# Two gated layers that turn unscaled rows and apply the row factor after the product; a norm and a copy moved inside the attention steps

## Chip, cores and metric

One core of one Trainium2 chip runs the whole program in one launch. The metric is the device time of that launch in microseconds (us); lower is better. The engines are named as the profile names them: PE (TensorE, the matrix engine; PEld is its weight load), ACT (ScalarE), DVE (VectorE), POOL (GpSimd) and SP (SyncE, which issues most of the DMAs).

## What is computed

Two transformer-like blocks on 256 tokens of width 1024, all in float32. The parts that matter here:

```
def rmsnorm(x, g):                       # y = x * rsqrt(mean(x*x) + EPS) * g
def swiglu(h, w_gu, w_down):
    gu = h @ w_gu                        # 1024 -> 2 x 2816
    g, u = jnp.split(gu, 2, axis=-1)
    return (jax.nn.silu(g) * u) @ w_down
f = swiglu(rmsnorm(h, ffn1_pre_g), ffn1_w_gu, ffn1_w_down);  h = h + 0.5 * rmsnorm(f, ffn1_post_g)
m = hybrid_mixer(rmsnorm(h, mix_pre_g), ...);                h = h + rmsnorm(m, mix_post_g)
c = memory_cross_attention(rmsnorm(h, xa_pre_g), ...);       h = h + rmsnorm(c, xa_post_g)
f = swiglu(rmsnorm(h, ffn2_pre_g), ffn2_w_gu, ffn2_w_down);  h = h + 0.5 * rmsnorm(f, ffn2_post_g)
```

Then a second block: another mixer and a layer that picks experts for each token. The hybrid mixer projects its input, runs a stick-breaking attention over 16 heads and a state-space scan beside it, normalises each (the state-space output `y * silu(z)` in two groups of 512), and multiplies both by `w_out`.

## The kernel before

**Products.** Tokens stand in two tiles of 128 (`tt` = 0, 1), the width in eight slices of 128 (`kt`). Every weight is streamed once from HBM by SP in 532 blocks of 128x1024 (512 KB) into a ring of four slots (`RING`). Each block is split in two: ACT copies it to `w_high` in PE's fast fp32r form (`split`, L496), DVE writes the rest to `w_low` (`split`, L1005), and PE does three products for each pair of operands (L1750 to L1752: high by high, low by high, high by low). SP loads a slot again as soon as `w_low` of the block in it is done (`w_split`).

**Entering a layer.** `pre_square` (ACT, L512) squares a tile of rows and sums it, then takes the root; `scaled` (DVE, L1027 and L1029) inverts that and writes the rows times the factor to `XN`; `turn_tile(k, tt)` (PE, L1757) turns the eight 128x128 squares of a tile of `XN` into PSUM; `highs` (ACT, L533) multiplies by the gain column and writes `xT_high`, `lows` (DVE, L1039) writes `xT_low`. `k` numbers the norms: 0 is the first gated layer, 3 the state-space norm, 6 the second gated layer. Before a norm that follows a residual update, `post_square` (ACT, L582) and `post_add` (DVE, L1084, L1090, L1092) norm the product in PSUM and add it to `H`, one tile after the other; `h_done` counts the updated tiles.

**The gated layer.** `ffn_up` makes eleven panels of 256 gates and 256 values. PE's first panel goes tile by tile (`panel_by_tile`): tile 0 through four weight blocks, then tile 1; `turn_after` says behind which block of tile 0 the second tile is turned (`None`: both are turned ahead of it). For each panel ACT writes `silu(gate)` (L549) and DVE multiplies by the value (L1055); PE turns the result back one panel later.

**The attention steps.** For `k` = 0 to 9, PE does `scores(k)` (L1924), `suffix_sums(k-1)` (L1941 to L1947), `weighted_values(k-2)` (L1959 to L1961), and half a panel of the projections that are still to come (panels 8 to 10 behind steps 1, 3 and 5; panel 9 holds keys that `scores(4)` needs). `attention_half(k, fill)` is the same step on ACT and on DVE, with one weight block split at `fill(0)` and one at `fill(1)`. On DVE it ends with `softplus_low` (L1192), for which `suffix_sums` waits. The state-space output is finished between these steps: `gated` (DVE, L1334) multiplies by the silu of `z`, the squares (ACT, L512), `scaled` and `panel(8)` follow step 1, `highs` and `lows` of norm 3 follow steps 2 and 3, and `panel(9)` comes behind those of step 3. `XN` and the scratch tile `XDD` share memory.

Every engine works through its own instructions in the order written, and semaphores tie them together.

Of the kernel before, what the change touches and what calls it, by code (L numbers as in the profile page):

```python
# [69 lines left out]

GATE_SCALE = 2.0 ** 14
# [32 lines left out]
def build(nc, stream, w_dt, cols, small_row, rows, x, mem, keys, out):  # L104
# [31 lines left out]
    STAT = sb("stat", [P, 64], 93.75)  # L136
    XAK = sb("xa_kT", [P, 8, SEQ], 97)
# [169 lines left out]
    eps_ok, rms_ok, xn_ok = sem("eps_ok"), sem("rms_ok"), sem("xn_ok")  # L307
# [44 lines left out]
    def _(sp):  # L352
        sp.dma_start(H[:, 0, :], x[0:P, :]).then_inc(x_in, 16)
        sp.dma_start(H[:, 1, :], x[P:SEQ, :]).then_inc(x1_in, 16)
        sp.dma_start(RING[:, 0, :], stream[0]).then_inc(loaded[0], 16)
        sp.dma_start(COLS[:], cols).then_inc(const_in, 16)
        for n in range(1, SLOTS):
            sp.dma_start(RING[:, n, :], stream[n]).then_inc(loaded[n], 16)
# [20 lines left out]
    def _(pool):  # L379
# [4 lines left out]
        pool.dma_start(ROWG[:], rows[0].partition_broadcast(P)).then_inc(row_in, 16)  # L384
# [4 lines left out]
        for mask, sign, compare, fill in ((UPTO, 1, ALU.is_ge, 0.0), (FROM, -1, ALU.is_ge, 0.0),  # L389
# [4 lines left out]
                               pattern=[[sign, P]], channel_multiplier=-sign).then_inc(masks_ok, 1)  # L394

# [60 lines left out]
        pool.wait_ge(xn_ok, 18)  # L456
# [29 lines left out]
    def _(act):  # L486
# [54 lines left out]
        def ffn_up(stage, f):  # L541
# [3 lines left out]
            def silu(p, parity, dyn=None):  # L545
                act.wait_ge(w_used, at(b + PB * (p + 1), dyn, PB))
                if dyn is not None or e + p >= 2:
                    act.wait_ge(hidden_done, at(e + p - 1, dyn))
                act.activation(SG[:, parity, :, :],  # L549
                               PAIR[parity].rearrange("p (t n) -> p t n", t=TT)[:, :, 0:256],  # L550
                               ACT.Silu).then_inc(silu_done, 1)
# [8 lines left out]
            split(b + PB, PB)  # L560
            silu(0, 0)
# [39 lines left out]
        act.wait_ge(eps_ok, 1)  # L601
        act.wait_ge(x_in, 16)
# [3 lines left out]
        split(0, 1)  # L606
        act.wait_ge(const_in, 16)
        highs(0, "ffn1", 0)
        split(1, 1)
        highs(0, "ffn1", 1)  # L610
        split(2, 2)
# [29 lines left out]

        def attention_half(k, fill):
# [8 lines left out]
            fill(1)  # L651
            if k < 8:
# [345 lines left out]
    def _(dve):  # L998
# [33 lines left out]

        def lows(k, gain, tt, high=XTH, low=XTL):
# [13 lines left out]
        def ffn_up(stage, f):  # L1047
            b, e = BASE[stage], f * FFN_PANELS

            def hidden(p, parity, dyn=None):  # L1050
                dve.wait_ge(silu_done, at(e + p + 1, dyn))
                if dyn is not None or e + p >= 2:

                    dve.wait_ge(ht_ps, at(e + p - 1, dyn))
                dve.tensor_tensor(HN[:, parity, :, :], SG[:, parity, :, :],  # L1055
                                  PAIR[parity].rearrange("p (t n) -> p t n", t=TT)[:, :, 256:512],
                                  ALU.mult).then_inc(hidden_done, 1)
# [7 lines left out]
            split(b + PB, PB)  # L1065
            hidden(0, 0)
# [46 lines left out]
        dve.wait_ge(x_in, 16)  # L1113
        scaled(0, H, 0)
        dve.wait_ge(x1_in, 16)
        scaled(0, H, 1)
        split(0, 1)
# [43 lines left out]

        def attention_half(k, fill):
# [159 lines left out]
        panel(7)  # L1322
# [1107 lines left out]
```

## Time and profile before

| | |
|---|---|
| median of 3 runs | 1722.03 us (1719.54 to 1722.96) |
| profiled execution | 1721.7 us, span 1720.0 us |
| mean granted TensorE clock | 0.989 of 2.4 GHz |
| busy share of the span | PE 97%, PEld 86%, DVE 69%, ACT 54%, POOL 7% |
| HBM | 284.86 MB read, 166 GB/s over the span |

The span is the profiled part of one execution. Times in the rows are us from its start. A row of the timeline gives start, duration, engine, line, operation, tiles, and in brackets how long the engine had been idle before it and what ended that.

### The profile page before, as it was taken

To read this page: it belongs to the slowest core of one execution; us is meant where nothing else is said; L and a number is where in the kernel's file an instruction comes from. 1 tells how busy PE (TensorE), PEld (TensorE's weight loads), DVE (VectorE), ACT (ScalarE), POOL (GpSimd) and SP (SyncE) were. 2 spreads that over 40 slices of the span, in tenths; PEclk is the share of its full clock that TensorE was granted. 3 is DMA by queue.
4 is the path that set the end of the run, shared out by engine and by line. 5 is a ranking of instruction groups with operands and counts; after the bars stand their busy time and mean duration, and the time that the engine had idled before them with its cause. 6 is when DMAs were issued, how large, how long until landed. Compare 5 with 4: busy or idle time off the path is not lost.

```text
span 1720.0 us, 30593 instructions
## 1 busy us (share of the span) xinstructions
PE 1672.3 (97%) x10346; PEld 1482.4 (86%) x10346; DVE 1190.6 (69%) x1827; ACT 934.2 (54%) x1540; POOL 114.5 (7%) x106
## 2 busy tenths in 40 slices
PE   7999999989998999999989999999999999999998
PEld 6888898889897788879979999999999888888887
DVE  5555687487666555466664799989999866666664
ACT  5445546476655544456354444467777654455554
POOL 0000004000000000010010000112222200000000
PEclk9999999989999999999999999999999999999999
DMA  7555453323453555645344455444444365665663
GB/s 260 186 183 183 171 196 123 111 97 124 153 190 123 171 183 184 192 144 187 125 163 158 161 169 195 169 162 146 147 147 148 132 209 193 195 193 190 192 194 122
DMA packets 78814, 286.79 MB, mean 167 GB/s; under 512 B 8864, under 2 KB 9120, under 8 KB 78624
## 3 DMA queue, kind: packets, MB, share of 16 engines
q1 hardware_dynamic: 77888, 282.27, 49.4%
q0 software_dynamic: 864, 3.67, 0.6%
q8 instruction: 41, 0.67, 0.2%
q14 instruction: 21, 0.17, 0.0%
HBM read 284.86 MB, written 1.05 MB: 166 GB/s over the span
## 4 chain that ended last, share of the span: by engine, by line
PE 79%; DVE 10%; issue 6%; ACT 4%; DVEq 1%; DMA 0%; ACTq 0%; POOL 0%; SPq 0%; POOLq 0%
PE ps L1750 24%; PE ps L1752 24%; PE ps L1751 24%; DVE one_at_key L1653 3%; DVE w_low L1005 3%; ACT gate_high_at_key L931 1%; DVE gate_low_at_key L1670 1%; ACT w_high L496 1%; PE ps L1757 1%; PE ps L1839 1%; DVE xT_low L1039 0%; DVE tmp L1090 0%; ACT xn L512 0%; PE ps L2276 0%; DVE h L1092 0%
## 5 line engine op out<-in xcount | busy, mean ns | idle before, releaser
L1005 DVE TENSOR_TENSOR w_low<-ring,w_high 128x1024 fp32r<-128x1024 f32 x532 | 654.2, 1232 | 341.4 <-ACT w_high L496 339.3
L496 ACT ACTIVATE w_high<-ring 128x1024 fp32r<-128x1024 f32 x532 | 559.4, 1056 | 319.2 <-PE ps L1752 312.4
L1750 PE MATMUL ps<-xT_high,w_high 128*128 128x256 f32 x1600 | 462.1, 289 | 1.9 <-DVE xT_low L1039 1.9
L1751 PE MATMUL ps<-xT_high,w_low 128*128 128x256 f32 x1600 | 454.2, 284 | 0.0
L1752 PE MATMUL ps<-xT_low,w_high 128*128 128x256 f32 x1600 | 454.1, 284 | 0.0
L1750 PEld LDWEIGHTS ps<-xT_high,w_high 128*128 128x128 f32 x1600 | 308.2, 193 | 5.9 <-DVE w_low L1005 2.3
L1751 PEld LDWEIGHTS ps<-xT_high,w_low 128*128 128x128 f32 x1600 | 308.4, 193 | 0.7 <-issue 0.5
L1752 PEld LDWEIGHTS ps<-xT_low,w_high 128*128 128x128 f32 x1600 | 308.0, 193 | 0.0
L1750 PE MATMUL ps<-w_high,expert_w_high 128*128 128x512 f32 x512 | 200.5, 392 | 0.4 <-DVE expert_w_low L1713 0.4
L1751 PE MATMUL ps<-w_high,expert_w_low 128*128 128x512 f32 x512 | 200.0, 391 | 0.0
L1752 PE MATMUL ps<-w_low,expert_w_high 128*128 128x512 f32 x512 | 200.0, 391 | 0.0
L1750 PE MATMUL ps<-w_high,xT_high 128*128 128x512 f32 x464 | 187.1, 403 | 11.5 <-DVE xT_low L1039 6.4
L1752 PE MATMUL ps<-w_low,xT_high 128*128 128x512 f32 x464 | 183.4, 395 | 0.0
L1751 PE MATMUL ps<-w_high,xT_low 128*128 128x512 f32 x464 | 183.4, 395 | 0.0
L980 ACT ACTIVATE expert_w_high<-expert_w 128x256 fp32r x124 | 51.8, 418 | 164.9 <-PE ps L1752 164.9
L1750 PEld LDWEIGHTS ps<-w_high,xT_high 128*128 128x128 f32 x464 | 88.7, 191 | 31.5 <-DVE w_low L1005 7.6
L1750 PEld LDWEIGHTS ps<-w_high,expert_w_high 128*128 128x128 f32 x512 | 96.6, 189 | 20.7 <-issue 0.6
L1751 PEld LDWEIGHTS ps<-w_high,expert_w_low 128*128 128x128 f32 x512 | 96.6, 189 | 19.9
L1752 PEld LDWEIGHTS ps<-w_low,expert_w_high 128*128 128x128 f32 x512 | 96.5, 189 | 19.9
L931 ACT ACTIVATE gate_high_at_key<-one_at_key,gate_high 128x128 f16<-128x128 f16 x256 | 82.0, 391 | 52.5 <-DVE one_at_key L1653 52.5
L1731 DVE TENSOR_TENSOR expert_w_low<-expert_w,expert_w_high 128x256 fp32r<-128x256 f32 x124 | 52.7, 425 | 82.3 <-ACT expert_w_high L980 82.3
L1752 PEld LDWEIGHTS ps<-w_low,xT_high 128*128 128x128 f32 x464 | 88.6, 191 | 19.1
(373 smaller groups left out, 2115.1 us busy)
## 6 DMA issues: line engine op xcount, KB each, us to landing
ring<-in_stream SPq DMA_DIRECT2D x532, 512.0 KB, 3.4
row_gain<-in_rows POOLq DMA_DIRECT2D x4, 512.0 KB, 4.4
h<-in_x SPq DMA_DIRECT2D x2, 512.0 KB, 4.3
mem_sb<-in_mem SPq DMA_DIRECT2D x1, 1024.0 KB, 11.3
keys_sb<-in_keys POOLq DMA_DIRECT2D x1, 1024.0 KB, 5.3
out<-result SPq DMA_DIRECT2D x2, 512.0 KB, 2.6
last_gain<-in_rows POOLq DMA_DIRECT2D x1, 512.0 KB, 4.8
cols<-in_cols SPq DMA_DIRECT2D x1, 78.5 KB, 7.4
```

The costliest lines, as they stand in the source:

```text
L496: act.activation(WH[:, n % SLOTS, :], RING[:, n % SLOTS, :], ACT.Copy).then_inc(w_high, 1)
L931: last = act.activation(OAH[:, g % 2, j, :], OAE[:, j // 2, :, j % 2], ACT.Copy, scale=gate)
L980: act.activation(WTH[:, v % 4, :], slot, ACT.Copy).then_inc(wt_high, 1)
L1005: dve.tensor_tensor(WL[:, n % SLOTS, :], RING[:, n % SLOTS, :], WH[:, n % SLOTS, :].bitcast(F32), ALU.subtract).then_inc(w_split, 1)
L1653: dve.tensor_tensor(OAE[:], IOTA16[:].unsqueeze(1).to_broadcast([P, GROUP // 2, P, 2]), pairs(KEY_T[:, 0, :], g, dyn), ALU.is_equal).then_ ...
L1670: dve.tensor_tensor(OAL[:, g % 2, :, :, :], OAE[:], pairs(GATE_LOW, g, dyn), ALU.mult).then_inc(low1_ok, 1)
L1731: dve.tensor_tensor(WTL[:, v % 4, :], slot, WTH[:, v % 4, :].bitcast(F32), ALU.subtract).then_inc(wt_low, 1)
L1750: pe.matmul(out, high, w_hi, start=start, stop=False, skip_group_check=True)
L1751: pe.matmul(out, low, w_hi, start=False, stop=False, skip_group_check=True)
L1752: return pe.matmul(out, high, w_lo, start=False, stop=stop, skip_group_check=True)
L1757: last = pe.transpose(xt_psum(k, tt)[:, kt, :], XN[:, tt, kt * P:(kt + 1) * P], IDENT[:])
L1839: last = pe.transpose(hidden_psum(p)[:, o:o + P], HN[:, parity, tt, ft * P:(ft + 1) * P], IDENT[:])
```

## The change

Four edits.

1. Both gated layers turn the rows of `H` as they are (no `scaled`). The factor of each row, 1/rms, goes to `ROW_FACTOR` (`row_factor` on DVE) and is applied behind the product: as the scale of the silu, and as the scalar of the multiplication that makes `hidden`. As the factor differs from tile to tile, each of the two becomes two instructions of 128x256 for a panel. The squares move behind `highs` of both tiles.
2. The order of the first loads: rows 0, the columns of gains, ring 0, ring 1, rows 1, then ring 2 and 3; the row gain (POOL's queue, 512 KB) waits until ring 3 has landed. The first gated layer turns its second tile behind block 0 of tile 0, the second gated layer behind block 2 (1 before). The splits of weight blocks move ahead of tile 1's `highs` and `lows`.
3. State-space norm: `gated(0)` goes behind `panel(7)`, `gated(1)` into step 0; the squares of tile `k` (`ssd_squares`) come ahead of step k's exponentials for k = 0 and 1, the roots (`ssd_roots`) behind step 1's.
4. `panel(9)`'s copies go ahead of `highs` and `lows` of the state-space norm's second tile.

```diff
@@ sync @@
         sp.dma_start(H[:, 0, :], x[0:P, :]).then_inc(x_in, 16)
+        sp.dma_start(COLS[:], cols).then_inc(const_in, 16)
+        sp.dma_start(RING[:, 0, :], stream[0]).then_inc(loaded[0], 16)
+        sp.dma_start(RING[:, 1, :], stream[1]).then_inc(loaded[1], 16)
         sp.dma_start(H[:, 1, :], x[P:SEQ, :]).then_inc(x1_in, 16)
-        sp.dma_start(RING[:, 0, :], stream[0]).then_inc(loaded[0], 16)
-        sp.dma_start(COLS[:], cols).then_inc(const_in, 16)
-        for n in range(1, SLOTS):
+        for n in range(2, SLOTS):
@@ gpsimd: row_gain's first load, moved behind the masks @@
+        pool.wait_ge(loaded[SLOTS - 1], 16)
         pool.dma_start(ROWG[:], rows[0].partition_broadcast(P)).then_inc(row_in, 16)
@@ scalar: ffn_up @@
-                act.activation(SG[:, parity, :, :],
-                               PAIR[parity].rearrange("p (t n) -> p t n", t=TT)[:, :, 0:256],
-                               ACT.Silu).then_inc(silu_done, 1)
+                for tt in range(TT):
+                    last = act.activation(SG[:, parity, tt, :], PAIR[parity][:, tt * 512:tt * 512 + 256], ACT.Silu,
+                                          scale=ROW_FACTOR[:, tt:tt + 1])
+                last.then_inc(silu_done, 1)
...
             split(b + PB, PB)
+            act.wait_ge(factor_ok, 2 * f + 2)
             silu(0, 0)
@@ scalar: start @@
+        act.wait_ge(const_in, 16)
+        highs(0, "ffn1", 0)
+        split(0, 4)
+        highs(0, "ffn1", 1)
         act.wait_ge(x_in, 16)
         pre_square(0, H, 0)
         act.wait_ge(x1_in, 16)
         pre_square(0, H, 1)
-        split(0, 1)
-        act.wait_ge(const_in, 16)
-        highs(0, "ffn1", 0)
-        split(1, 1)
-        highs(0, "ffn1", 1)
-        split(2, 2)
@@ scalar: attention @@
+        def ssd_squares(tt):
+            act.wait_ge(y_used, 2)
+            act.wait_ge(y_done, tt + 1)
+            for g in range(2):
+                w, n = slice(g * 512, g * 512 + 512), 2 * tt + g
+                chain(act.activation(XN[:, tt, w], YS[:, tt, w], ACT.Square, accum_out=STAT[:, n:n + 1]))
+        def ssd_roots():
+            chain(act.activation(STAT[:, 4:8], STAT[:, 0:4], ACT.Ln, scale=1.0 / 512,
+                                 bias=STAT[:, EPS_COL:EPS_COL + 1]))
+            act.activation(STAT[:, 8:12], STAT[:, 4:8], ACT.Exp, scale=-0.5).then_inc(rms_ok, 2)
...
             fill(1)
+            if k < 2:
+                ssd_squares(k)
...
+            if k == 1:
+                ssd_roots()
...
-            if k == 1:
-                for tt in range(TT):
-                    act.wait_ge(y_done, tt + 1)
-                    pre_square(3, YS, tt, 2, log=True)
-            elif k in (2, 3):
-                highs(3, "ssd", k - 2, YTH)
+            if k == 2:
+                highs(3, "ssd", 0, YTH)
             if k in (1, 3, 5):
                 panel(8 + k // 2)
+            if k == 3:
+                highs(3, "ssd", 1, YTH)
@@ scalar: second gated layer @@
         split(b, 4)
         post_square(2, 0)
-        split(b + 4, 2)
+        split(b + 4, 3)
+        highs(6, "ffn2", 0)
+        post_square(2, 1)
+        split(b + 7, 1)
+        highs(6, "ffn2", 1)
         updated_square(6, 0, 4)
-        post_square(2, 1)
-        highs(6, "ffn2", 0)
         updated_square(6, 1, 4)
-        split(b + 6, 1)
-        highs(6, "ffn2", 1)
-        split(b + 7, 1)
@@ vector @@
+        def row_factor(k, tt):
+            dve.wait_ge(rms_ok, 2 * k + tt + 1)
+            dve.reciprocal(ROW_FACTOR[:, tt:tt + 1], STAT[:, 4 + tt:5 + tt]).then_inc(factor_ok, 1)
...
-                dve.tensor_tensor(HN[:, parity, :, :], SG[:, parity, :, :],
-                                  PAIR[parity].rearrange("p (t n) -> p t n", t=TT)[:, :, 256:512],
-                                  ALU.mult).then_inc(hidden_done, 1)
+                for tt in range(TT):
+                    last = dve.scalar_tensor_tensor(HN[:, parity, tt, :], PAIR[parity][:, tt * 512 + 256:tt * 512 + 512],
+                                                    ROW_FACTOR[:, tt:tt + 1], SG[:, parity, tt, :], ALU.mult, ALU.mult)
+                last.then_inc(hidden_done, 1)
@@ vector: start (both scaled(0, ...) are gone) @@
         dve.wait_ge(const_in, 16)
         lows(0, "ffn1", 0)
-        split(1, 1)
+        split(0, 4)
         lows(0, "ffn1", 1)
-        split(2, 2)
+        row_factor(0, 0)
+        row_factor(0, 1)
@@ vector: attention (gated(0) now stands behind panel(7), ahead of the wait for y_ps 3) @@
                 dve.scalar_tensor_tensor(SPL[:, k % 2, :], ZS[:, k % 2, :], -1.0, ZS[:, k % 2, :],
                                          ALU.mult, ALU.min).then_inc(abs_done, 1)
+            if k == 0:
+                gated(1)
...
             if k == 1:
-                gated(0)
-                gated(1)
-                dve.wait_ge(y_done, 2)
                 scaled(3, YS, 0, 2, log=True)
                 scaled(3, YS, 1, 2, log=True)
-            elif k in (2, 3):
-                lows(3, "ssd", k - 2, YTH, YTL)
+            elif k == 2:
+                lows(3, "ssd", 0, YTH, YTL)
             if k in (1, 3, 5):
                 panel(8 + k // 2)
+            if k == 3:
+                lows(3, "ssd", 1, YTH, YTL)
@@ vector: second gated layer @@
         split(b, 4)
         post_add(2, 0, 1.0)
-        split(b + 4, 1)
-        updated_scale(6, 0, 4)
-        split(b + 5, 1)
+        split(b + 4, 2)
+        lows(6, "ffn2", 0)
+        split(b + 6, 1)
         post_add(2, 1, 1.0)
-        lows(6, "ffn2", 0)
-        updated_scale(6, 1, 4)
-        split(b + 6, 2)
+        split(b + 7, 1)
         lows(6, "ffn2", 1)
+        row_factor(6, 0)
+        row_factor(6, 1)
@@ tensor @@
         def turn_tile(k, tt):
-            pe.wait_ge(xn_ok, 2 * k + tt + 1)
+            if k == 0:
+                pe.wait_ge(ident_ok, 1)
+                pe.wait_ge(x1_in if tt else x_in, 16)
+            elif k == 6:
+                pe.wait_ge(h_done, 5 + tt)
+            else:
+                pe.wait_ge(xn_ok, XN_OK[k] + tt + 1)
+            rows = H if k in (0, 6) else XN
...
-        turn_tile(0, 1)
-        ffn_up("ffn1_up", 0, 0, None)
+        ffn_up("ffn1_up", 0, 0, 0)
...
-        ffn_up("ffn2_up", 1, 6, 1)
+        ffn_up("ffn2_up", 1, 6, 2)
```

## Rows read from the trace of the kernel before

**Rows 1.** Waits of PE over the whole span: us in total, times, longest.
```profile
PE ps L1757 <- DVE xn L1029: 13.6, 5, 7.5
PE ps L1750 <- DVE xT_low L1039: 8.3, 4, 3.3
PE ps L1750 <- DVE w_low L1005: 5.3, 4, 2.6
```

**Rows 2.** Timeline of the start.
```profile
4.83 1.06 ACT L512 ACTIVATE xn<-h 128x1024 f32<-128x1024 f32 x1 [2.74 <-DMA h<-in_x]
...
7.52 3.65 PE L1757 MATMUL ps<-ident,xn 128*128 128x128 f32 x16 [7.52 <-DVE xn L1029]
...
8.51 1.06 ACT L496 ACTIVATE w_high<-ring 128x1024 fp32r<-128x1024 f32 x1 [0.84 <-DMA ring<-in_stream]
9.59 2.17 ACT L533 ACTIVATE xT_high<-ps,cols 128x128 fp32r<-128x128 f32 x8
...
10.83 2.16 DVE L1039 SCALAR_TENSOR_TENSOR xT_low<-ps,cols,xT_high 128x128 fp32r<-128x128 f32 x8
...
17.38 0.50 PE L1750 MATMUL ps<-w_high,xT_high 128*128 128x512 f32 x1 [1.54 <-DVE w_low L1005]
```

**Rows 3.** Stretches: length, busy us of PE, PEld, DVE, ACT, POOL, granted clock, DMA share, GB/s.
```profile
368.20:376.80 8.60, 8.60 (x39) 8.60 (x40) 7.50 (x15) 6.50 (x12) 0.00 (x0) 0.50 0.35 124
...
557.70:564.50 6.80, 5.25 (x12) 4.02 (x13) 4.91 (x12) 2.41 (x5) 0.53 (x1) 0.50 0.44 155
...
569.60:577.00 7.40, 7.40 (x33) 6.11 (x34) 4.92 (x11) 3.39 (x4) 0.00 (x0) 1.00 0.30 99
```

**Rows 4.** Timeline of attention steps 0 to 4, by engine: ACT, then DVE, then PE.
```profile
341.76 0.85 ACT L656 ACTIVATE softplus<-softplus 128x768 f32<-128x768 f32 x1 [1.88 <-DVE softplus L1169]
...
343.52 0.96 DVE L1185 SCALAR_TENSOR_TENSOR softplus<-scores,softplus 128x768 f32<-128x768 f32 x1 [1.79 <-ACT softplus L657]
...
353.74 2.35 DVE L1334 TENSOR_TENSOR ssd_out<-ssd_out,projections 128x1024 f32<-128x1024 f32 x2
...
358.99 0.88 DVE L1029 TENSOR_SCALAR xn<-ssd_out,stat 128x512 f32<-128x512 f32 x2 [0.98 <-ACT stat L518]
...
367.13 0.95 DVE L1192 TENSOR_TENSOR softplus_low<-softplus,softplus_high 128x768 fp32r<-128x768 f32 x1
...
368.18 0.66 PE L1944 MATMUL ps<-softplus_high,from_r 128*128 128x384 f32 x1 [4.05 <-DVE softplus_low L1192]
...
372.90 1.91 PE L1757 MATMUL ps<-ident,xn 128*128 128x128 f32 x8
...
382.32 0.71 PE L1924 MATMUL ps<-projections 64*128 64x256 f32 x4 [0.83 <-ACT projections L539]
```

**Rows 5.** Timeline at the entry of the second gated layer, DVE, then PE.
```profile
551.00 1.23 DVE L1092 SCALAR_TENSOR_TENSOR h<-tmp,h 128x1024 f32<-128x1024 f32 x1
...
554.85 1.09 PE L1757 MATMUL ps<-ident,xn 128*128 128x128 f32 x8 [1.51 <-DVE xn L1029]
559.25 0.76 PE L1750 MATMUL ps<-w_high,xT_high 128*128 128x512 f32 x1 [3.30 <-DVE xT_low L1039]
...
569.58 0.50 PE L1750 MATMUL ps<-w_high,xT_high 128*128 128x512 f32 x1 [2.63 <-DVE w_low L1005]
```

**Rows 6.** Page, costliest groups: weight block on DVE, and two of 128x256.
```profile
L1005 DVE TENSOR_TENSOR w_low<-ring,w_high 128x1024 fp32r<-128x1024 f32 x532 | 654.2, 1232 | 341.4 <-ACT w_high L496 339.3
...
L980 ACT ACTIVATE expert_w_high<-expert_w 128x256 fp32r x124 | 51.8, 418 | 164.9 <-PE ps L1752 164.9
...
L1731 DVE TENSOR_TENSOR expert_w_low<-expert_w,expert_w_high 128x256 fp32r<-128x256 f32 x124 | 52.7, 425 | 82.3 <-ACT expert_w_high L980 82.3
```

**Rows 7.** View of the tile silu_gate: ns min/median/max, first and last start.
```profile
L549 ACT ACTIVATE silu_gate<-ps x22: 579/580/597, 28.3 to 690.9; 128x512 f32<-128x512 f32 x22
```

**Rows 8.** Timeline of PE and DVE at the end of the first gated layer.
```profile
144.74 0.60 PE L1839 MATMUL ps<-ident,hidden 128*128 128x128 f32 x4
...
141.32 0.68 DVE L1055 TENSOR_TENSOR hidden<-silu_gate,ps 128x512 f32<-128x512 f32 x1
```

More of the change, by code:

```diff
@@ L68 @@
 HG_CHUNK = 32
+XN_OK = {k: 2 * sum(j not in (0, 6) for j in range(k)) for k in range(9)}
 GATE_SCALE = 2.0 ** 14
@@ L136, in build @@
     STAT = sb("stat", [P, 64], 93.75)
+    ROW_FACTOR = STAT[:, 12:14]
     XAK = sb("xa_kT", [P, 8, SEQ], 97)
@@ L306, in build @@
     act_chain, dve_chain = sem("act_chain"), sem("dve_chain")
-    eps_ok, rms_ok, xn_ok = sem("eps_ok"), sem("rms_ok"), sem("xn_ok")
+    eps_ok, rms_ok, xn_ok, factor_ok = sem("eps_ok"), sem("rms_ok"), sem("xn_ok"), sem("row_factor_ok")
     xt_ps, xt_high, xt_low = sem("xT_psum"), sem("xT_high_done"), sem("xT_low_done")
@@ L383, in _ @@
                            pattern=[[-1, P]], channel_multiplier=1).then_inc(ident_ok, 1)
-        pool.dma_start(ROWG[:], rows[0].partition_broadcast(P)).then_inc(row_in, 16)
         for mask in (UPTO, FROM, BEFORE, CAP, ONES):
@@ L394, in _ @@
                                pattern=[[sign, P]], channel_multiplier=-sign).then_inc(masks_ok, 1)
+        pool.wait_ge(loaded[SLOTS - 1], 16)
+        pool.dma_start(ROWG[:], rows[0].partition_broadcast(P)).then_inc(row_in, 16)
         def row_gain(k):
@@ L455, in _ @@
         pool.wait_ge(iota_ok, 1)
-        pool.wait_ge(xn_ok, 18)
+        pool.wait_ge(xn_ok, XN_OK[8] + 2)
         pool.memset(GE[:, 105:, :], 1.0).then_inc(slots_one, 1)
@@ L1065, in ffn_up @@
             split(b + PB, PB)
+            dve.wait_ge(factor_ok, 2 * f + 2)
             hidden(0, 0)
@@ L1112, in _ @@
         dve.memset(STAT[:, EPS_COL:EPS_COL + 1], EPS).then_inc(eps_ok, 1)
[L1113 to L1117, printed above, removed]
         dve.wait_ge(const_in, 16)
         lows(0, "ffn1", 0)
-        split(1, 1)
+        split(0, 4)
         lows(0, "ffn1", 1)
-        split(2, 2)
+        row_factor(0, 0)
+        row_factor(0, 1)
         dve.wait_ge(small_in, 32)
@@ L1160, in over_diagonals, with gated @@
             return mask[:].unsqueeze(1).unsqueeze(1).to_broadcast([P, 2, 2, P])
+        def gated(tt):
+            dve.wait_ge(y_used, tt + 1)
+            dve.wait_ge(z_silu, 2)
+            y = YS[:, tt, :]
+            dve.tensor_tensor(y.rearrange("p (a n) -> p a n", a=2), y.rearrange("p (a n) -> p a n", a=2),
+                              Z[:, :, tt, :], ALU.mult).then_inc(y_done, 1)
         def attention_half(k, fill):
@@ L1322, in _ @@
         panel(7)
+        gated(0)
         dve.wait_ge(y_ps, 3)
@@ L1328, in _ @@
         dve.tensor_tensor(YS[:, 1, :], YS[:, 1, :], XDD[:], ALU.add).then_inc(y_used, 1)
-        def gated(tt):
-            dve.wait_ge(y_used, tt + 1)
-            dve.wait_ge(z_silu, 2)
-            y = YS[:, tt, :]
-            dve.tensor_tensor(y.rearrange("p (a n) -> p a n", a=2), y.rearrange("p (a n) -> p a n", a=2),
-                              Z[:, :, tt, :], ALU.mult).then_inc(y_done, 1)
         for k in range(10):
@@ L1339, in _ @@
             if k == 1:
-                gated(0)
-                gated(1)
-                dve.wait_ge(y_done, 2)
                 scaled(3, YS, 0, 2, log=True)
                 scaled(3, YS, 1, 2, log=True)
-                dve.wait_ge(xn_ok, 8)
-            elif k in (2, 3):
-                lows(3, "ssd", k - 2, YTH, YTL)
+                dve.wait_ge(xn_ok, XN_OK[3] + 2)
+            elif k == 2:
+                lows(3, "ssd", 0, YTH, YTL)
             if k in (1, 3, 5):
                 panel(8 + k // 2)
+            if k == 3:
+                lows(3, "ssd", 1, YTH, YTL)
             elif k == 7:
@@ L1754, in turn_tile @@
         def turn_tile(k, tt):
-            pe.wait_ge(xn_ok, 2 * k + tt + 1)
+            if k == 0:
[6 more added lines that the diff above has]
+            rows = H if k in (0, 6) else XN
             for kt in range(KT):
-                last = pe.transpose(xt_psum(k, tt)[:, kt, :], XN[:, tt, kt * P:(kt + 1) * P], IDENT[:])
+                last = pe.transpose(xt_psum(k, tt)[:, kt, :], rows[:, tt, kt * P:(kt + 1) * P], IDENT[:])
                 if kt % 4 == 3:
```

## The prediction

> **What bounds the kernel now.** I read the page's busy shares first (PE 97% of the span), then the list of what PE waited for, then the timeline around each wait that the diff touches. PE sets the time, so only PE's idle time, and stretches in which its clock is low, can be won. Three rows of waits hold most of that idle time: on `xn`, on `xT_low` and on `w_low`, 27.2 us in all [rows 1]; a fourth, before `suffix_sums(2)`, is 4.05 us [rows 4]. Beside them stands a cost that no wait shows: after a gap PE runs at the lower of its two clock levels, 1.2 GHz. PE idled 4.05 us, and from there to 376.8 the granted clock is 0.50; at the entry of the second gated layer it idled 1.51 and 3.30 us within six, and 557.7 to 564.5 is at 0.50 [rows 3, 5].
>
> **Unit costs.** PE at full clock starts a 512-wide product about every 0.227 us (7.40 us hold 33 of them [rows 3]); six of them, one weight block for one token tile, take 1.36 us, and a first panel (48) 10.9 us. Eight turns take about 0.9 us at full clock (1.09 with the drain of the last [rows 5]) and twice that at 0.50 (1.91 [rows 4]). Eight `highs` take 2.17 us, eight `lows` 2.16, a `w_high` 1.06, a `w_low` 1.23, of which 1.15 before the next can follow [rows 2, 6].
>
> **Start.** Before, rows 0 land at 4.83, squares, root, inverse and `scaled` put the first turn at 7.52, and the first block's `w_high` waits for ring 0 until 8.51. The panel runs without a gap only from 17.38, when 12 of its 48 products are done, so it ends at 17.38 + 36 x 0.227 = 25.5 [rows 2].
> After: no scaling. Rows 0 now share the engines with less (the row gain and rows 1 come later), so they land at 4.3 to 4.8; turns follow, four turns at 1.2 GHz are 0.9 us, `highs` of tile 0 run from 5.6 to 7.8, `w_high` of blocks 0 to 3 to about 12.0, and `w_low` of block 0 is done at 10.2. DVE's chain then is 1.15 us a block, to 13.7. PE does block 0 from 10.2, turns tile 1, and finds every block ready behind it. At full clock it would end at 10.2 + 10.9 + 0.9 + about 1.2 of waits = 23.2, a gain of 2.3. The columns' DMA (78.5 KB, now second in SP's queue) has to be there by 5.6; it is small and has one transfer ahead of it. Rows 1 and the three blocks need 2.1 MB more by 11.5; 4.5 us of this kernel's 400 GB/s and more would carry it, so they are in time. The row gain waits on POOL's queue, with only the waits for `h_done` and the state-space work of much later behind it.
> But the clock: the 16 turns of before take 3.65 us, 0.23 us each, the price of the lower level, while the first product at 11.6 already runs at full rate. In the new order PE works 1.8 us, idles some 3.5, then starts block 0. I take block 0 and the second turns at 1.2 GHz (1.36 + 0.9 = 2.3 us more at most) and 1.0 us of it net, since part of it fills the waits for `w_low`. Gain 1.3 us; bounds 0.3 and 2.5.
> The Trainium skill ("TensorE: Matmul & The Clock Gate", "What's actually happening") says that the throttled level is the default and that activity releases it. The trace agrees (0.23 us a turn at the start, 0.11 later), and by the rule the early turns buy no warm clock, where a reading by waits alone would give 2.3.
>
> **The gated layers' panels.** Silu goes from one instruction of 0.58 us to two, the product with the value from one of 0.68 to two [rows 7]. The nearest 128x256 rows are 0.42 and 0.43 us [rows 6], so +0.26 on ACT and +0.18 on DVE for each of 22 panels, 9.7 us of engine time. On the path it costs nothing: PE turns `hidden` one whole panel (11 us) later, and where the cover is thinnest, the last panel, DVE begins the product at 141.32 and PE wants it at 144.74 [rows 8], 2.7 us after it is done; 0.44 fits. Without that cover it would be 22 x 0.44 = 9.7 us. The squares and the two inverses, about 3 us on ACT, now lie ahead of the second panel's splits: at the start they end by 18 and the panel is wanted at 24; in the second layer they end around 567.1, block 4 is split by 569.3, and PE wants it at 569.3. I count 0.1.
>
> **Attention steps.** Removed from behind step 1 on DVE: `gated` twice (2.35), the wait for the squares and roots, which kept the last `scaled` until 359.9; there remain four half rows of 0.44 (0.88 for two [rows 4]). DVE ends `softplus_low` of step 1 at 353.7 [rows 4], 0.2 later by what comes in step 0; 1.9 of `scaled` and 0.6 of `panel(8)` put its step 2 at 356.5 against 360.5, 4.0 us earlier.
> Where the work goes: `gated(0)` (1.22) into a wait of 0.96 before the carry product, 0.2 left over; `gated(1)` into DVE's wait of 1.79 for the logarithm; the squares of a tile (1.5 us, an estimate from the 1.06 of a row square [rows 2] cut in two with its readouts) into ACT's waits for `abs`, 1.88 in step 0 [rows 4]; the roots (0.6) into ACT's wait before `softplus_high`. So step 0 costs 0.2.
> Step 2's own chain on DVE (block, `abs`, `log_attention`, logarithm, `softplus`, block, `softplus_low`) ran 360.5 to 368.0, 7.5 us; from 356.5 it ends near 363.9. PE wants it at 364.13 (368.18 - 4.05) + 0.2, so the 4.05 us are gone, by 0.4. Before, PE's work from there to `scores(4)` ran 368.18 to 381.49 (382.32 - 0.83), 13.3 us, of which 8.6 at 0.50 [rows 3, 4]; at full clock those are 4.3 and the whole is 9.0: PE is at `scores(4)` at 373.4. Step 3 on DVE takes 2.2 (`lows`) + 7.5 + 0.7 (`panel(9)`, now ahead of the second `lows`), to 374.4, so PE waits 1.0 there (0.83 before). `scores(4)` moves from 382.32 to 374.5. The second `lows` now lie behind it, and `softplus_low` of step 4 is ready 0.4 after PE wants it in step 5. Gain 7.8 - 0.4 = 7.4; bounds 3.5 (half of the stall stays and the clock falls again) and 8.
>
> **Second gated layer.** Before: PE's last product of the layer ahead ends at 553.34 (554.85 - 1.51), its first panel has 48 products and two turns, 12.6 us, so 566.0 is the ideal; it ended at 569.58 + 30 x 0.227 = 576.4. The 10.4 lost are 7.4 of waits (1.51 + 3.30 + 2.63) and the stretch at 0.50 [rows 3, 5].
> After: `h` of tile 0 is ready at 552.2 [rows 5], before PE is free, so the turn starts at 553.34; `highs` 554.0 to 556.2; `lows` from 555.2, the first two slices at 555.8: block 0 starts at 555.9, not 559.25. Blocks 0 and 1 follow on; block 2's `w_low` stands behind the `lows` on DVE and is done at 558.6, when PE arrives; PE is through it at 560.0. `post_add` of tile 1 stands behind that `w_low`: 558.6 + 0.2 + 1.25 + 1.25 = 561.3. PE waits 1.35, turns until 562.2, waits 0.3 for block 3 (`w_low` behind `post_add`), and ends tile 0 at 563.9; tile 1 has its first `lows` at 563.8. End 563.9 + 5.4 = 569.3, less the 0.1 above. Gain 7.0; bounds 4 (the clock falls at these shorter gaps as well, 1.7 a time, and the second turn is late) and 8.
>
> **Sum.** 1.3 + 7.4 + 7.0 = 15.7 us. The profiled execution took 1721.7 (span 1720.0), so 1706.0; the median of the runs lies 0.3 above it: 1706.3. The low-clock stretches in places that the diff leaves alone shift with the rest; one more or one fewer is worth some 2 us.
>
> **Rivals.**
> - *The stall in the attention steps only moves.* For it: my margin is 0.4 us, and DVE is busy 7.50 of 8.60 us behind the stall [rows 3]; steps 3 and 4 hold the same work. Then PE waits some 2 us before `suffix_sums(2)` or at `scores(4)` and the clock falls again: 3.5 instead of 7.4, 1710.2.
> - *The second gated layer keeps part of its loss.* For it: two waits of 1.7 and 1.35 remain, and 1.51 and 3.30 were followed by 6.8 us at 0.50. Against it: the gap of 2.63 at 567 was followed by 7.40 us at 1.00 [rows 3, 5]. It costs 3: 1709.3. With the first rival, 1713.2. The Trainium skill (same page, "HAM oscillation — how this bites in real kernels") tells of short bursts between waits that keep PE falling back to the low clock; the trace has one case of each kind.
> - *The halved silu and product are exposed.* 9.7 us, 1716.0. Against it: the slack of 2.7 us [rows 8].
> - *The start or a clock stretch elsewhere comes out better*: 2.5 instead of 1.3 and one stretch of 0.50 fewer, 1702.
> - *Nothing is gained*: the waits on `xn` are replaced by waits on `w_low` of the same length in all three places. 1722. The chain on DVE loses real instructions, which speaks against it.
> - *Slower.* PE turns once, falls idle and begins the panel cold; if the clock stayed at 1.2 GHz, each 2 us would cost 1. The three gains are eaten at 34 us of low clock (15.7 + 1.3, doubled), three panels; at 50 us the time is 1706.3 + 25 - 1 = 1730. For it: at 368.2 PE was busy and yet had 0.50 for 8.6 us [rows 3]. Against it: no stretch here is longer.
>
> **Chances.** Forecast (1702.5 to 1709) 0.56; attention stall moves 0.14; second layer keeps half 0.10; both 0.05; exposed halves 0.03; better 0.06; nothing gained 0.04; slower 0.02. 1700.5 to 1712.8 leaves out most of "both" and the last cases, and a tail of "better", under 2 in 10. A measurement of this kernel tells 0.2% (3.4 us) from no change: faster 0.94, same 0.04, slower 0.02.
>
> **What would show it.** Right: `silu_gate` and `hidden` with 44 instructions of about 0.42 us; no wait of PE on `xn` at the start or near 545; first product at about 10, first panel done near 24; no wait over 1 us at `suffix_sums(2)`; no 0.50 between 364 and 377; `scores(4)` some 9 us earlier in the span; 15.9 us from the last product ahead of the second gated layer to its first panel's end (23.0 before). Wrong: waits on `w_low` in those places, ACT idle behind `y_used` in step 0, or low clock in the first two panels or after the 1.35 us gap.

## The result, and the profile after

The changed kernel took 1707.15 us (median of five runs, 1706.76 to 1713.11) against 1722.03 (1719.54 to 1723.5): a ratio of 0.9928, 95% interval 0.9909 to 0.9946. Two further series gave 1706.42 (0.9922, 0.9909 to 0.9936) and 1710.63 (0.9936, 0.9922 to 0.9950). The forecast was 1706.3, with a range of 1702.5 to 1709: the first two medians lie in it, the third lies 1.6 above it. The profiled execution took 1707.15, span 1705.4, 14.6 us shorter than the span before.

All 16 runs of the changed kernel lie in two groups: nine at 1706.3 to 1707.2 with a mean granted clock of 0.993 or 0.994, seven at 1710.4 to 1713.1 with 0.989 to 0.992. Their cause is taken up with the experiments.

What PE waited for, over the whole span (us in total, times, longest):

```profile
PE ps L1777 <- DVE xT_low L1066: 6.5, 3, 2.6
PE ps L1792 <- DMA h<-in_x: 4.8, 1, 4.8
PE ps L1792 <- DVE xn L1051: 4.6, 3, 2.6
...
PE ps L1777 <- DVE w_low L1027: 4.0, 2, 3.9
...
PE ps L1958 <- ACT projections L545: 1.0, 1, 1.0
...
PE ps L1792 <- DVE h L1121: 0.9, 1, 0.9
```

The wait on `xn` fell from 13.6 us to 4.6 [rows 1] (what is left belongs to other norms), and the wait on `softplus_low` is not in the list any more. New are a wait for rows 0 and one of 0.9 for `h`.

The start, PE and ACT:

```profile
4.79 1.94 PE L1792 MATMUL ps<-ident,h 128*128 128x128 f32 x8 [4.79 <-DMA h<-in_x]
6.00 2.18 ACT L539 ACTIVATE xT_high<-ps,cols 128x128 fp32r<-128x128 f32 x8 [3.90 <-PE ps L1792]
...
10.60 0.79 PE L1777 MATMUL ps<-w_high,xT_high 128*128 128x512 f32 x1 [3.87 <-DVE w_low L1027]
11.19 0.63 PE L1778 MATMUL ps<-w_high,xT_low 128*128 128x512 f32 x1
...
13.32 1.91 PE L1792 MATMUL ps<-ident,h 128*128 128x128 f32 x8
...
15.56 0.39 PE L1779 MATMUL ps<-w_low,xT_high 128*128 128x512 f32 x1
```

A product takes 0.63 us until 15.3 and 0.39 from there, and a row of eight turns 1.91, as at 0.50 before [rows 4]: block 0 and tile 1's turns ran at 1.2 GHz, as forecast.

The attention steps (PE and DVE) and the entry of the second gated layer (PE, DVE):

```profile
350.49 0.95 DVE L1227 TENSOR_TENSOR softplus_low<-softplus,softplus_high 128x768 fp32r<-128x768 f32 x1
351.35 1.67 DVE L1051 TENSOR_SCALAR xn<-ssd_out,stat 128x512 f32<-128x512 f32 x4
...
360.28 0.95 DVE L1227 TENSOR_TENSOR softplus_low<-softplus,softplus_high 128x768 fp32r<-128x768 f32 x1
361.67 0.44 PE L1978 MATMUL ps<-softplus_high,from_r 128*128 128x384 f32 x1
...
372.00 0.71 PE L1958 MATMUL ps<-projections 64*128 64x256 f32 x4 [1.01 <-ACT projections L545]
...
543.34 1.03 PE L1792 MATMUL ps<-ident,h 128*128 128x128 f32 x8
545.90 0.47 PE L1777 MATMUL ps<-w_high,xT_high 128*128 128x512 f32 x1 [1.54 <-DVE xT_low L1066]
...
549.87 1.23 DVE L1121 SCALAR_TENSOR_TENSOR h<-tmp,h 128x1024 f32<-128x1024 f32 x1
551.15 1.09 PE L1792 MATMUL ps<-ident,h 128*128 128x128 f32 x8 [0.90 <-DVE h L1121]
552.29 0.50 PE L1777 MATMUL ps<-w_high,xT_high 128*128 128x512 f32 x1
```

`softplus_low` of step 2 is done at 361.2, and `suffix_sums(2)` starts at 361.67 without a wait; `scores(4)` waits 1.01 (0.83 before [rows 4]). In the second gated layer the three waits of 1.51, 3.30 and 2.63 [rows 5] are 1.54 and 0.90. And the clock stayed up (stretches: length, busy us of PE, PEld, DVE, ACT, POOL, granted clock, DMA share, GB/s):

```profile
364.20:372.00 7.80, 6.79 (x59) 6.61 (x58) 7.43 (x9) 5.58 (x10) 0.00 (x0) 1.00 0.28 78
...
546.00:553.00 7.00, 6.05 (x29) 4.65 (x30) 6.17 (x11) 3.56 (x10) 0.53 (x1) 1.00 0.57 175
```

**Where the 14.6 us are**, by the shift of one event in each stage between the two traces: ACT's first square behind the first gated layer from 196.20 to 195.17 (1.0); up to the state-space scan 2.6 (so 1.6 more, in a stretch that the diff doesn't touch: 0.50 for 3.4 us from 254.1, where it was 6.8 us from 253.9); behind the attention steps, the next such square from 462.85 to 453.00, 9.85 (7.25 more); the first turn of `hidden` in the second layer from 587.42 to 570.15, 17.3 (7.4 more); and at the last squares from 1708.59 to 1694.03, 14.6: 2.7 given back in the expert layer.

Only 0.9 of those 2.7 us are low clock (6.8 us at 0.50 from 1346.4, where the kernel before has 3.4). Another 1.7 are lost ahead of that, at full clock, on the same 1928 products. The stretch between two of PE's waits for `gate_high_at_key`, the changed kernel and then the kernel before (columns as above):

```profile
1127.50:1343.80 216.30, 213.55 (x1928) 201.66 (x1928) 214.87 (x302) 157.01 (x362) 66.31 (x60) 1.00 0.44 145
1144.60:1359.40 214.80, 212.76 (x1928) 201.66 (x1928) 214.00 (x302) 157.05 (x362) 63.26 (x60) 1.00 0.43 146
```

It takes 216.3 to 216.5 us in all eleven profiles of kernels that turn unscaled rows, and 214.8 to 214.9 in the three that don't (before, kernels 1 and 3 below). So this loss comes with the new gated layers every time, and not with the halved instructions, which kernel 3 has. PE's gaps ahead of the products of `gate_high_at_key` grow by 0.03 to 0.2 us now and then; the diff touches no line of this layer, and what makes them grow stays open.

### The profile page after: what moved, and what is told of

It reads as the page before. It is cut to its first block, busy times and chain, and to the rows that moved or that the text cites. A ratio compares the mean times of both kernels' runs of the same rounds, so it can differ in the third digit from the quotient of the medians.

```text
span 1705.4 us, 30633 instructions
## 1 busy us (share of the span) xinstructions
PE 1667.1 (98%) x10346; PEld 1476.0 (87%) x10346; DVE 1192.4 (70%) x1845; ACT 938.7 (55%) x1560; POOL 117.6 (7%) x106
## 4 chain that ended last, share of the span: by engine, by line
PE 81%; DVE 9%; issue 6%; ACT 3%; DVEq 1%; ACTq 0%; DMA 0%; POOL 0%; POOLq 0%
PE ps L1777 25%; PE ps L1779 25%; PE ps L1778 25%; DVE one_at_key L1680 3%; DVE w_low L1027 2%; ACT gate_high_at_key L953 1%; PE ps L1792 1%; DVE gate_low_at_key L1697 1%; PE ps L1874 1%; ACT w_high L502 0%; DVE xT_low L1066 0%; PE ps L2310 0%; PE ps L2154 0%; PE ps L2016 0%; PE ps L2034 0%
## 6 DMA issues: line engine op xcount, KB each, us to landing
cols<-in_cols SPq DMA_DIRECT2D x1, 78.5 KB, 3.6
```

## The experiments

Kernel 1 is that of experiment 1, and so on; kernel 10 has the narrow products spread as well, kernel 11 has not. All times stand beside runs of the kernel before on the same chip. A stage is measured between the events just named.

**1. Attention edits alone** (edits 3 and 4 on the kernel before).

> The kernel before with edits 3 and 4 alone (state-space norm in steps 0 and 1, panel 9's copies ahead of the second highs and lows). Theory (the three gains add up, each in its own place): 7.2 us faster than before, 1714.5 to 1715, no PE wait over 1.1 us in the attention steps, and no 0.50 stretch between 364 and 377; the PE waits on xn at 7.5 and 553 as in rows 2 and 5. Rival (the steps gained only because the start had shifted the chip's clock stretches): the wait of 4.05 us is gone but a stretch of low clock of 6.8 us or more comes at the wait of 1 us ahead of scores(4), and only 4 us are gained.

Measured: 1715.13 against 1721.73, ratio 0.9965 (0.9952 to 0.9979), 6.6 faster. The stage from the scan to the square behind the attention steps took 126.63 us, 133.86 before, 126.61 in the changed kernel. The theory holds: 7.2 us, independent of the other edits. The profiled execution was the slowest of the five (1718.2, granted clock 0.988); its low clock lies outside the attention steps, none of it between 259 and 548 us.

**2. Gated layers alone** (the changed kernel with edits 3 and 4 undone).

> The changed kernel with edits 3 and 4 undone: unscaled rows, first loads and the new orders in the two gated layers alone. Theory: 1.0 us at the start and 7.3 in the second layer, 8.3 faster than before, 1713.7; the 4.05 us wait ahead of suffix_sums(2) stays, with 8 to 10 us of low clock behind it. Rival (the three places share one gain, since low-clock stretches move between them): under 5 us faster, with more low clock than before outside the attention steps.

Measured: 1713.99, ratio 0.9963 (0.9950 to 0.9977), 7.7 faster, for 8.3 expected. The wait of 4.1 on `softplus_low` is back, and the granted clock is 0.50 for 6.8 us with it (8 to 10 expected). 6.6 + 7.7 = 14.3 of the 15.3 us that the changed kernel had in the same series (1721.73 - 1706.42): the places add up within what the clock leaves uncertain.

**3. The halves alone.**

```diff
-                act.activation(SG[:, parity, :, :], PAIR[parity]...[:, :, 0:256], ACT.Silu)
+                for tt in range(TT):
+                    act.activation(SG[:, parity, tt, :], PAIR[parity][...], ACT.Silu, scale=ROW_FACTOR[:, tt:tt + 1])
...
+        dve.memset(ROW_FACTOR, 1.0).then_inc(factor_ok, 1)
```

The product with the value on DVE is halved in the same way.

> The kernel before with silu and hidden as two instructions of 128x256 for each panel, with a factor of 1.0 for every row (so nothing is normalised in another way). Theory (hidden behind PE): within 1 us of before, ACT and DVE busier by 22 x 0.35 and 22 x 0.27 us, no new wait of PE. Rival (exposed): 22 x 0.6 = 13 us slower if each panel's turn waits, 0.6 to 1.2 slower if only the last panel of each layer does.

Measured: 1721.40 against 1721.73, ratio 1.0001 (0.9992 to 1.0010), 11 runs. The views of the tiles `silu_gate` and `hidden` in this kernel (ns min/median/max):

```profile
L551 ACT ACTIVATE silu_gate<-ps,stat x44: 454/463/475, 28.1 to 690.1; 128x256 f32<-128x256 f32 x44
L1059 DVE SCALAR_TENSOR_TENSOR hidden<-ps,stat,silu_gate x44: 473/477/486, 29.0 to 691.4; 128x256 f32<-128x256 f32 x44
```

Each is 0.05 us dearer than I had taken from 128x256 rows of other operations, 0.35 on ACT and 0.27 on DVE for a panel, and none of it shows: hidden.

**4. Turns of the identity at the start** (on the changed kernel; nobody reads their output).

```diff
+        warm(14)                       # 14 x pe.transpose(PS[:, 1024:1152], IDENT, IDENT)
         turn_tile(0, 0)
+        warm(20)
         ffn_up("ffn1_up", 0, 0, 0)
```

> The changed kernel with turns of the identity that nobody reads: 14 before the first real turn (from 1.6 to about 4.8 us, where PE only waits for rows 0) and 20 between the turns of tile 0 and the first block (from 6.7, where PE waited 3.87 us for w_low). Nothing else changes. Theory (the start's missing 1.3 us of the 2.3 that waits alone would give are low clock, since PE had fallen idle before block 0): block 0 and the second turns run at 2.4 GHz, the first panel ends 1.0 to 1.4 us earlier, 1705.2 to 1705.5 against 1706.4. Rival (the start is bound by w_low and by the second tile's highs, not by the clock): within 0.3 us, with the time moved into waits; or later, where the idle turns are still running when w_low is done.

Measured: 1711.30 (1709.92 to 1711.44), ratio 0.9936. Both expectations missed that. It is also the ratio of the changed kernel's own series on the same chip (1710.63, 0.9936, experiment 8): by medians the turns neither gained nor lost, and a loss stands only against the lower group of the changed kernel's times. PE at the start of this kernel:

```profile
1.60 3.15 PE L1939 MATMUL ps<-ident 128*128 128x128 f32 x14 [1.60 <-POOL ident L387]
4.67 1.07 PE L1792 MATMUL ps<-ident,h 128*128 128x128 f32 x8
5.58 2.35 PE L1939 MATMUL ps<-ident 128*128 128x128 f32 x20
10.03 0.50 PE L1777 MATMUL ps<-w_high,xT_high 128*128 128x512 f32 x1 [2.10 <-DVE w_low L1027]
...
13.84 0.63 PE L1778 MATMUL ps<-w_high,xT_low 128*128 128x512 f32 x1
```

The real turns ran at the higher level (1.07 for eight), but 20 were over at 7.9, PE paused 2.1 us, and the clock fell again at 11.4. Still the first layer ended 0.4 to 1.0 us earlier than in the changed kernel's profiles. What is lost against a profile of the lower group lies far behind it, in places that no edit touches; the granted clock of those stretches:

```profile
250.30:260.50 10.20, 10.20 (x38) 9.04 (x38) 8.26 (x26) 1.07 (x4) 0.00 (x0) 0.50 0.15 51
803.30:806.70 3.40, 3.40 (x18) 3.40 (x17) 3.01 (x11) 0.28 (x1) 0.00 (x0) 0.51 0.45 154
868.10:878.30 10.20, 7.69 (x35) 7.32 (x36) 7.00 (x19) 5.65 (x17) 5.01 (x1) 0.50 0.68 249
```

In the changed kernel's profiled execution the same places have 3.4 us, none, and 6.8:

```profile
254.30:257.70 3.40, 3.40 (x10) 2.69 (x9) 3.24 (x12) 0.46 (x2) 0.00 (x0) 0.53 0.00 0
865.30:872.10 6.80, 4.46 (x22) 4.09 (x21) 5.78 (x16) 4.24 (x12) 4.40 (x1) 0.51 0.64 242
```

By stages, against that execution, it is 3.2 us behind panel 2, 1.8 in the second mixer and 1.0 at the expert layer's entry, with 0.9 won back in the expert layer.

**5. Without edit 4** (panel 9's copies again behind the second tile's `highs` and `lows`).

> The changed kernel with panel 9's copies again behind highs and lows of the norm's second tile. Theory (by the queues: ACT ends those highs about 366.4 + 2.2 and is free before panel 9 is done at 370.9, but DVE would do 2.2 us of lows first, of which it has the inputs only at 368 to 370, behind softplus_low at 371.2): panel 9's copy on DVE at 373.4 instead of 371.2, scores(4) 2.2 us later, 1.5 to 2.2 us slower: 1708.3. Rival (no need of edit 4: DVE has the lows done before panel 9): within 0.3 us.

Measured: 1714.66 (1708.3 expected), ratio 0.9960 (0.9947 to 0.9974); the attention stage took 132.55 us instead of 126.61. Timeline, DVE and PE:

```profile
370.77 2.16 DVE L1066 SCALAR_TENSOR_TENSOR ssd_outT_low<-ps,cols,ssd_outT_high 128x128 fp32r<-128x128 f32 x8
372.85 0.68 DVE L1072 COPY projections<-ps 128x512 f32<-128x512 f32 x1
...
373.63 1.23 PE L1958 MATMUL ps<-projections 64*128 64x256 f32 x4 [3.11 <-issue]
```

The copy starts 1.6 us later than in the changed kernel (372.85 against 371.21, with the start 0.4 earlier), the wait ahead of `scores(4)` is 3.1 instead of 1.0, and then the granted clock is 0.50 for 10.2 us. The expectation had the wait right and left out the clock. In this stage edit 4 is worth 5.9 us, of which the wait is 2.1 and the rest goes with the low clock: without it the stall of before moves by one step, as my first rival had it.

**6. Old order in the second gated layer, rows still unscaled.**

```diff
-        split(b + 4, 3)                 # ACT
-        highs(6, "ffn2", 0)
-        post_square(2, 1)
+        split(b + 4, 2)
+        updated_square(6, 0, 4)
+        post_square(2, 1)
+        highs(6, "ffn2", 0)
...
-        lows(6, "ffn2", 0)              # DVE
-        split(b + 6, 1)
         post_add(2, 1, 1.0)
+        lows(6, "ffn2", 0)
...
-        ffn_up("ffn2_up", 1, 6, 2)
+        ffn_up("ffn2_up", 1, 6, 1)
```

> The changed kernel with the second gated layer's queues in the order of before (post_square and post_add of tile 1 ahead of highs and lows of tile 0, the squares between, second turn behind block 1), but with unscaled rows. Theory (the 7.3 us come mostly of the order, not of the scaling that is gone): tile 0 is turned at 543.3 as in the changed kernel, its lows start only behind post_add of tile 1, first product near 548.5 instead of 545.9, and the second turn is late too: 3 to 5 us slower than the changed kernel, about 1710.5. Rival (it comes of the missing scaling): within 1 us.

Measured: 1717.54 (11 runs, 1712.90 to 1718.66; some 1710.5 expected), ratio 0.9972. From the last square ahead of the layer to its first turn of `hidden`: 39.52 us, against 39.48 before and 32.06 in the changed kernel. Timeline, PE:

```profile
544.08 1.03 PE L1792 MATMUL ps<-ident,h 128*128 128x128 f32 x8
549.48 0.76 PE L1777 MATMUL ps<-w_high,xT_high 128*128 128x512 f32 x1 [4.36 <-DVE xT_low L1067]
...
558.93 0.50 PE L1777 MATMUL ps<-w_high,xT_high 128*128 128x512 f32 x1 [2.65 <-DVE w_low L1028]
```

Turning unscaled rows lets the turn start without a wait and gives nothing by itself: the 1.51 us come back in the wait for `lows`, 4.36 instead of 3.30, with a turn that is done sooner. Those `lows` stand behind `post_add` of tile 1 on DVE. With unscaled rows, then, the order makes all of the 7.4 us. Whether the new order would give as much with scaled rows was not tried, so it isn't shown that the order needs no help from the missing scaling.

The wait of 2.65 at 558.93 shows something more. In the kernel before and in kernel 3 the same wait (2.63) was followed by full clock, and my prediction leaned on that. Here it was followed by low clock, and in kernel 1 too (2.65 at 560.44, then 0.50 from 561.9 to 565.3):

```profile
559.60:563.00 3.40, 3.40 (x10) 2.62 (x9) 1.48 (x8) 0.00 (x0) 0.00 (x0) 0.51 0.42 154
```

**7. Old order of the first loads.**

> The changed kernel with the first loads in the order of before (rows 0, rows 1, ring 0, columns, rings 1 to 3, and the row gain at once on POOL's queue). Theory (the columns land 7.4 us after their issue as in before, near 9.6): highs of tile 0 start 3.6 us later than at 6.0, block 0 at 14 instead of 10.6, while the second tile's turn no longer waits; 2.5 to 3.5 us slower, 1709.4, all the gain of the start and more. Rival (the order of the loads does nothing, ACT and DVE set the pace): within 0.5 us.

Measured: 1713.96 (1709.4 expected), ratio 0.9952. The first layer ended 3.0 us later than in the changed kernel. ACT and PE:

```profile
9.64 2.18 ACT L537 ACTIVATE xT_high<-ps,cols 128x128 fp32r<-128x128 f32 x8 [7.54 <-DMA cols<-in_cols]
...
14.24 0.79 PE L1775 MATMUL ps<-w_high,xT_high 128*128 128x512 f32 x1 [7.54 <-DVE w_low L1025]
```

The columns, 78.5 KB, land 7.3 us after their issue, behind three loads of 512 KB; in the changed kernel, behind one, it is 3.6. Without this edit the start is 2.0 us slower than before (198.16 against 196.20). The row gain is back in POOL's queue at once in this kernel too; the two were not tried apart.

**8. The changed kernel again, twice.**

> The changed kernel once more, for its two groups of times (1706.8 to 1707.2 in three of five runs, 1712.2 and 1713.1 in two; mean clock 0.993 and 0.989 to 0.990). Theory: the groups differ by low-clock stretches of PE alone, which fall where the gaps lie against the chip's own rhythm; a profile of the slower group shows the same waits and one or two more stretches at 0.50, about 10 us of them for 5 us. Rival: the slower group has a longer wait on a DMA or on the second layer's h.

> The changed kernel a third time, beside the three below, so that its two groups of times (1706.3 to 1707.2 in seven of ten runs, 1711.0 to 1713.1 in three) and theirs come from the same hours of the same chip. Theory (where the low-clock stretches fall changes from one execution to the next, with the same program): both groups again. If the profiled execution is of the slower group, its granted clock shows more and longer stretches at 0.50, in the narrow products at 250, in the state chunks at 800 and at the entry of the expert layer at 865. Rival (the slower runs have another cause): the same stretches and a longer wait.

Both profiles fell in the lower group (span 1704.6, four stretches at 0.50 ahead of the last squares, of 3.4, 3.4, 6.8 and 6.8 us, as in the first). No execution of the upper group of this kernel was profiled. The upper group was one of five executions on the one chip (1706.42) and four of six on the other (1710.63), where kernels 4 to 7 and 9 to 11 ran.

**9. The narrow products spread.** These are the products that make `dt` for the state-space scan, behind panel 2. They are 48 products of 16 columns, not 96 as the expectation says: two tiles, eight slices, three products each. In the changed kernel they start every 0.11 us from 248.61 to 253.78.

```diff
-        for n in range(3):
-            mix(n)
...
+        for b in range(PB):
+            mix(2, range(b, b + 1))
+            last = dt_products(b // 2, range(b % 2 * 4, b % 2 * 4 + 4))
```

> The changed kernel with the 96 narrow products for dt (16 columns each, 5.5 us in one row behind panel 2) cut into four parts, one behind each block of panel 2. Theory (the stretch at 0.50 that follows them in every profile, 3.4 to 10.2 us long, comes of these products in a row, not of a wait, since PE is busy through it): no low clock near 250, 1.6 to 4.9 us less between the first dt product and the scan, 1704.7 for the faster group. Rival (the low clock comes of them however they lie, or the later dt delays DVE's conv): within 0.5 us or slower.

Measured: 1709.85 (1709.35 to 1710.39, all at 0.993 or 0.994), ratio 0.9931. In its trace:

```profile
239.00:263.00 24.00, 21.09 (x158) 19.76 (x157) 19.66 (x47) 8.57 (x11) 0.00 (x0) 1.00 0.34 116
263.80:267.20 3.40, 3.40 (x10) 2.62 (x9) 3.37 (x7) 0.00 (x0) 0.00 (x0) 0.50 0.36 105
```

The theory on the clock holds in this profile and in that of kernel 10: with wide products between them, the narrow ones bring no low clock. The total that it gave, 1704.7, was missed: `dt` no longer has the half panel of cover behind it, PE waits 2.9 us for `ssd_small`, the clock falls there for as long as it does in the changed kernel's profiles (3.4 us), and the kernel is 3.4 us slower than the median of the changed kernel's lower group (1706.42). None of its five runs is in an upper group, and against the changed kernel's series on the same chip (1710.63) it is not told apart.

**10 and 11. More turns at the start** (14 and 34), with the narrow products spread and without.

> Both: the narrow products spread, and turns of the identity at the start, 14 before rows 0 and 34 (20 in the earlier kernel) between tile 0's turns and block 0, so that PE has no pause of 2.1 us ahead of block 0 as it had with 20. Theory: the sum, 1.6 from the narrow products and 1.0 to 2.3 from the start, 1702.5 to 1703.8 for the faster group. Rival (the start's gain is eaten by turns still running when w_low is done, at 10.0): no faster than the kernel with the spread alone.

> The changed kernel with 14 and 34 turns of the identity at the start and nothing else. Theory (the 1711.3 of the kernel with 20 came of low-clock stretches far behind the start, the start itself being 0.4 to 1.0 us shorter): the start is 1.0 to 2.0 us shorter than in the changed kernel, no 0.50 between 5 and 15, and the total 1704.5 to 1705.5 in the faster group, with a slower group 5 us above. Rival (turns at the start make the total slower, whatever the start does): 1710 or more in all runs.

Measured: 1706.85 (1702.5 to 1703.8 expected; ratio 0.9917, 0.9904 to 0.9930), and 1708.50 (six runs, 1704.59 to 1710.34; 0.9918, 0.9904 to 0.9933). PE at the start of the second one:

```profile
5.96 3.88 PE L1939 MATMUL ps<-ident 128*128 128x128 f32 x34
10.41 0.50 PE L1777 MATMUL ps<-w_high,xT_high 128*128 128x512 f32 x1 [0.57 <-DVE w_low L1027]
11.91 1.04 PE L1792 MATMUL ps<-ident,h 128*128 128x128 f32 x8
```

The pause ahead of block 0 is 0.57 us, block 0 and the second turns run at the higher level, and the first layer ends at 193.06 instead of 194.56 to 195.17 (1.5 to 2.1 us), with the spread at 192.83 instead of 194.88 (2.0). The two runs of kernel 11 at 0.994 took 1704.6, 1.7 less than the lowest of the changed kernel's: the shortest times of all. Its other four, at 0.989 to 0.991, took 1708.1 to 1710.3. By medians neither is told apart from the changed kernel.

**The two groups.** Kernel 11 was profiled in one of its slower executions (1708.91, clock 0.990). Against the third profile of the changed kernel (0.994) it won 1.6 us at the start and was 2.6 later at the last squares, so 4.2 lost between: 1.6 in the narrow products (low clock 6.8 instead of 3.4 us), 0.7 and 1.5 in the second mixer, 1.2 at the entry of the expert layer (10.2 instead of 6.8), 0.8 won back in the expert layer. Its waits behind the start are those of that profile to within 0.2 us each, but for one of 0.5 for `expert_w_low` that is not in the other's list. The Trainium skill ("TensorE: Matmul & The Clock Gate", "What's actually happening") says that the activity monitor runs freely and does not begin anew with a kernel; with that it fits that one program has mean granted clocks of 0.994 and of 0.990 from one execution to the next. But no run here shows the stretches themselves differ for one program: the three profiles of the changed kernel have the same four lengths. That its seven slower runs come of longer stretches rests on their mean clocks, not on a profile. The two stretches that mark kernel 4's and kernel 11's profiles, 3.4 us at 801 to 811 and 10.2 us at 866 to 876, are in those of kernels 1, 5 and 7 as well, which differ in other places, and in none of the other nine profiles. So no edit is shown to bring them. Why all five runs of kernel 4 and none of kernel 9 are of that kind stays open; with four of six executions of the unchanged program of that kind on the same chip, five of five may be chance.

## Why the prediction was right, by its steps

- **Start, 1.3 forecast, 1.0 measured** (to 1.6 in the other profiles). First product at 10.60 instead of 10.2, since rows 0 landed at 4.79, the late end of my range, and `highs` began at 6.00 instead of 5.6. Block 2 of the ring came 1.0 us after ACT wanted it, which PE did not feel. The clock's part had the right sign and was put too low: I took 1.0 net, and kernels 10 and 11 give 1.5 to 2.1 us back by keeping PE busy.
- **Halves, 0 forecast, 0.0 measured** (ratio 1.0001). The 44 instructions of each kind take 0.466 and 0.477 us in the changed kernel, for 0.42 and 0.43 forecast; the cover of a whole panel hides that too.
- **Attention, 7.4 forecast, 7.25 measured** (7.2 alone). `softplus_low` of step 2 was 0.4 ahead by my sum and 0.44 by the trace (360.28 + 0.95 against 361.67); the wait at `scores(4)` 1.0 and 1.01; at `suffix_sums(4)` 0.4 and 0.5. The margin decides: without edit 4 the wait is 3.1, the clock falls, and only 1.3 of the 7.25 stay.
- **Second gated layer, 7.0 forecast, 7.4 measured.** From the turn to the end of the first panel 15.96 by the sum; by the trace 552.29 + 30 x 0.227 - 543.34 = 15.8. The second wait was 0.90 instead of 1.35, and the clock did not fall. What I had not seen is that the missing scaling gives nothing here without the new order. And my argument that the clock would stay up, full clock behind the wait of 2.63, was weaker than it looked: kernels 1 and 6 have low clock behind the same wait.
- **Sum, 15.7; the three places together 15.7.** The span differs by 14.6 because a shorter clock stretch behind panel 2 won 1.6 and the expert layer lost 2.7. Of these, 0.9 are a longer clock stretch; 1.7 are a loss at full clock that comes with the new gated layers, a term that my sum did not have at all. The prediction had put one stretch more or fewer at 2 us; that size was right (3.4 us at half the clock are 1.7), and such stretches are probably also why medians of one kernel differ by 4 us between series.
- **Luck.** That the median came within 0.9 us of 1706.3 is in part luck: the missing 1.7 was nearly made up by the 1.6 behind panel 2, and three of the five executions were of the lower group. In the third series four of six were not, and its median, 1710.63, is above my range.

## What to carry to other kernels

Take a stalled tile's chain apart by queue: here removing the scaling gave nothing at the second gated layer while its neighbours kept their old order, and with unscaled rows the order of a few queue entries carried 7 us. Count the clock with the wait: the single waits of 1.0 us ahead of `scores(4)` had no low clock behind them in ten profiles, those of 2.65 us had it in two of four, and 2.1 us more of waiting ahead of `scores(4)` cost 5.9. A small table that everything waits for goes second in the load queue, ahead of the weights. And after a change, compare stages that it does not touch as well: 1.7 us were lost in one of them in every profile.

## Unexpected in the hardware

- PE can show as busy all the time and still fall to 1.2 GHz: within or right behind 48 products of 16 columns in a row (one every 0.11 us, each drawn as 0.26 us) the granted clock went to 0.50 for 3.4 to 10.2 us in twelve profiles, and not in the two with wide products between them. The ends of products are modelled in the profile, so a row without gaps is no proof of an array at work all the time.
- Turns of the identity raised the clock like real work: with 14 of them from 1.60 us on the real turns from 4.67 ran at the higher level, and a pause of 2.1 us (busy from 10.03 on) was followed by 0.50 from 11.4.
- The same wait was followed by full clock in two kernels (2.63 us, before and kernel 3) and by 3.4 us at 0.50 in two others (2.65 us, kernels 1 and 6).
- One program on one chip took 1706.3 us in two executions and 1710.4 to 1712.9 in four. The slower kind of this program was not profiled; the profiles of kernels 1, 4, 5, 7 and 11, with clocks of 0.988 to 0.991, share a stretch at 0.50 at 801 to 811 us and a longer one than the others at 866 to 876.
